# A hybrid decoder step on one core: samples' sums kept in four groups of eight rows to the end, and the first stages' expert loads issued one step later

## The reference, cut to what matters

```python
def decoder_layer(x, ...):
    mix, new_conv, new_ret = token_mixer(rmsnorm(x, norm_mix), ...)   # x @ w_in, short convolution, retention, @ w_out
    h = x + mix
    return h + moe(rmsnorm(h, norm_ffn), w_router, b_router, w_up, b_up, w_down, b_down), new_conv, new_ret

def moe(xn, ...):                       # 264 tokens, top 4 of 32 experts
    h = xb @ w_up[e] + b_up[e]          # 1024 -> 2048, rows of the tokens of expert e
    act = glu(h)                        # clamped SwiGLU
    y = act @ w_down[e] + b_down[e]     # 1024 -> 1024
    return sum over the token's 4 experts of gate * y

y_prompt = rmsnorm(hp)   # 256 prompt rows of 1024
y_sample = rmsnorm(hs)   # 8 sample rows of 1024
```

## Time and profile before

| | before |
|---|---|
| median of 3 runs | 1088.58 us |
| lowest, highest | 1085.95, 1090.34 us |
| the profiled execution | 1085.15 us |
| its span in the trace | 1083.2 us |
| TensorE busy | 1065.2 us (98%) |
| VectorE busy | 361.7 us (33%) |
| ScalarE busy | 152.6 us (14%) |
| read from HBM, written | 427.00 MB, 3.48 MB |
| mean rate over the span | 397 GB/s |

### The profile page before, as it was taken

The page is one execution under the profiler, slowest core; times in us unless marked ns, Lnnn a source line. Parts: engine busy times, 40 slices in busy tenths (PEclk is TensorE's granted clock), DMA queues, the critical chain, the costliest instruction groups (busy, mean ns, idle before and its releaser), DMA issues.

```text
span 1083.2 us, 13193 instructions
## 1 busy us (share of the span) xinstructions
PE 1065.2 (98%) x5692; PEld 446.5 (41%) x5693; DVE 361.7 (33%) x572; ACT 152.6 (14%) x302; POOL 11.9 (1%) x28
## 2 busy tenths in 40 slices
PE   9999999999999999999999999999999999999997
PEld 7888664333333333333333333333333333333332
DVE  3376534233332223333322222323332232232234
ACT  2121144101111110111111111011111101011113
POOL 1000010000000000000000000000000000000002
PEclk9999999999999999999999999999999999999999
DMA  8975949999999999999999999999999999999994
GB/s 292 312 276 198 407 161 381 412 428 426 433 434 427 433 431 430 431 429 431 433 429 428 434 431 428 430 432 431 429 430 434 430 429 430 426 427 427 430 415 177
DMA packets 40907, 431.47 MB, mean 398 GB/s; under 512 B 4456, under 2 KB 19852, under 8 KB 25104
## 3 DMA queue, kind: packets, MB, share of 16 engines
q1 hardware_dynamic: 40240, 430.41, 94.8%
q10 hardware_dynamic: 608, 0.20, 0.1%
HBM read 427.00 MB, written 3.48 MB: 397 GB/s over the span
## 4 chain that ended last, share of the span: by engine, by line
PE 83%; DMA 15%; SPq 1%; issue 0%; ACT 0%; DVE 0%; ACTq 0%; POOLq 0%; DVEq 0%; POOL 0%
PE bank L1015 37%; PE bank L1034 15%; DMA ring_all<-in_w_up 14%; PE bank L695 8%; PE bank L1079 6%; PE bank L989 4%; PE bank L1026 2%; PE bank L805 2%; PE bank L997 2%; PE bank L1007 1%; PE bank L1072 1%; PE bank L1091 1%; PE bank L813 1%; DMA ring_all<-in_w_in 1%; SPq L516 1%; PE bank L648 1%
## 5 line engine op out<-in xcount | busy, mean ns | idle before, releaser
L1015 PE MATMUL bank<-ring_all,work 128*64 128x512 f32 x2048 | 484.6, 600 | 7.7 <-DMA ring_all<-in_w_up 7.7
L1015 PEld LDWEIGHTS bank<-ring_all,work 128*64 128x64 f32 x2048 | 134.7, 136 | 257.4 <-issue 247.9
L1034 PE MATMUL bank<-ring_all,work 128*64 128x512 f32 x992 | 225.3, 596 | 0.0
L1847 DVE TENSOR_TENSOR h_tok<-h_tok,bank 128x1024 f32<-128x1024 f32 (+1 forms) x67 | 81.8, 1221 | 236.6 <-PE bank L1079 230.7
L1034 PEld LDWEIGHTS bank<-ring_all,work 128*64 128x64 f32 x992 | 68.4, 137 | 129.1 <-issue 128.2
L695 PE MATMUL bank<-work,ring_all 128*128 128x264 f32 x384 | 87.0, 387 | 1.0 <-DMA ring_all<-in_w_in 1.0
L1817 DVE TENSOR_TENSOR work<-bank,bias_up 128x1024 f32<-128x1024 f32 x32 | 39.2, 1224 | 124.0 <-PE bank L1026 124.0
L695 PEld LDWEIGHTS bank<-work,ring_all 128*128 128x128 f32 x384 | 72.5, 190 | 13.4 <-DMA ring_all<-in_w_in 1.4
L1079 PE MATMUL bank<-work 64*128 64x512 f32 (+1 forms) x268 | 75.1, 637 | 0.0
L1834 DVE TENSOR_TENSOR work<-work 128x512 f32<-128x512 f32 x32 | 22.2, 693 | 108.8 <-ACT work L1419 108.8
L1403 ACT ACTIVATE work<-bank 128x264 f32<-128x264 f32 x32 | 12.5, 390 | 315.9 <-PE bank L1007 315.9
(11 more groups left out here) (236 smaller groups left out, 549.0 us busy)
## 6 DMA issues: line engine op xcount, KB each, us to landing
ring_all<-in_w_up SPq DMA_DIRECT2D x48, 4096.0 KB, 32.8
ring_all<-in_w_down SPq DMA_DIRECT2D x24, 4096.0 KB, 33.9
ring_all<-in_w_up SPq DMA_DIRECT2D x30, 2048.0 KB, 38.1
ring_all<-in_w_down SPq DMA_DIRECT2D x13, 2048.0 KB, 40.5
ring_all<-in_w_in SPq DMA_DIRECT2D x13, 1024.0 KB, 5.1
ring_all<-in_w_down SPq DMA_DIRECT2D x6, 1024.0 KB, 21.8
ring_all<-in_w_out SPq DMA_DIRECT2D x4, 1024.0 KB, 11.7
ring_all<-in_w_up SPq DMA_DIRECT2D x4, 1024.0 KB, 6.1
```

What stands on the lines that cost most here:

```text
L1015: mm = pe.matmul(bank[half * CAP:(half + 1) * CAP, up_bank(n) + b, :].rearrange("q (k p) -> q p k", k=KT), x, src[:, half * FF + b * 512:h ...
L1034: mm = pe.matmul(bank[half * CAP:(half + 1) * CAP, Y, :], av[:, 2 * i + k, :], src[:, k * D + half * 512:k * D + (half + 1) * 512], start= ...
L1847: tt(rows, rows, bank[0:m, b:b + 2, :], ALU.add).then_inc(comb_added, 1)
```

## The change

What it does:

- SP: chunk k of the experts is issued at j = 5 + 2k instead of 3 + 2k, so chunks 0 to 5 go out at j = 5 to 15. The wait for `summed` moves with chunk 5 to j = 15, and `store_states` now stands behind chunk 5. The router's weights move to j = 5. The two b_up loads and the copy of the convolution's state move behind the whole loop.
- Samples: `FOLD` is gone. `combine`, `bias` and `combine_last` always use the form with four groups of rows, DVE adds to `sums`, and b_down's product for the samples is eight matmuls in place of two. At n = 0 eight more products with `ident` bring the samples' rows of `h_tok` into the groups.
- End: the order of the last sums is samples, tile 0, tile 1 (`LASTS`) in the second half. The samples' squares lie in four groups of rows; two products with a constant 0/1 matrix (`same_row`) add them across the groups (`join_rows`), ahead of the branch for overflow. The final norm's load is issued after chunk 186 is used and lands in that chunk's slot, with the matrix and four small pieces of the norm for the groups (`fin_in`, six DMAs). The stores are tile 0, two groups of the samples, tile 1 on SP, and two groups of the samples on ACT.

The diff, cut to its core:

```diff
@@ SP
-                    if j >= 3:
-                        k = (j - 3) // 2
-                        if j == 13:
+                    if j >= 5:
+                        k = (j - 5) // 2
+                        if j == 15:
                             sp.wait_ge(summed, 5)
-                        elif j == 15:
-                            store_states(sp)
                         if j % 2 and k < FIRST - 1:
                             sp.dma_start(ring_a[:, k, :], chunk_src(stream[k])).then_inc(landed[k], 16)
-                        if j == 3:
+                        if j == 5:
                             sp.dma_start(w_rt[:], w_router[0].rearrange("(k p) e -> p k e", p=P)).then_inc(misc_in, 16)
-                            for half, p0 in enumerate(BU):
-                                sp.dma_start(x_tok[p0:p0 + E, 2, :], b_up[0, :, half * FF:(half + 1) * FF]).then_inc(bu_in, 16)
-                            sp.dma_start(conv_sample[0, :, 0, :], state_conv[0, :, 1, :]).then_inc(out_done, 16)
+                        if j == 15:
+                            store_states(sp)
...
                 sp.dma_start(b_rt[:], b_router.partition_broadcast(P)[:, 0, :]).then_inc(b_rt_in, 16)
+                for half, p0 in enumerate(BU):
+                    sp.dma_start(x_tok[p0:p0 + E, 2, :], b_up[0, :, half * FF:(half + 1) * FF]).then_inc(bu_in, 16)
+                sp.dma_start(conv_sample[0, :, 0, :], state_conv[0, :, 1, :]).then_inc(out_done, 16)
...
-                sp.wait_ge(comb_psum, CT * (FOLD + 1))
+                sp.wait_ge(mm_done, LATE + 1)
+                sp.dma_start(same_row, c_square[:, 8, :]).then_inc(fin_in, 16)
                 sp.dma_start(g_fin[:], norm_final.rearrange("(a d) -> a d", a=1)
-                             .partition_broadcast(P)[:, 0, :]).then_inc(late_in, 16)
+                             .partition_broadcast(P)[:, 0, :]).then_inc(fin_in, 16)
+                for g in range(4):
+                    sp.dma_start(g_fold[32 * g:32 * g + NS], norm_final.rearrange("(a n g t) -> g a n t", a=1, n=2, g=4)[g]
+                                 .partition_broadcast(NS)[:, 0]).then_inc(fin_in, 16)
@@ PE, combine
-                    if c == 2 and isinstance(n, int) and n < FOLD:
+                    if c == 2:
+                        if isinstance(n, int) and n == 0:
+                            for g in range(4):
+                                for half in range(2):
+                                    pe.matmul(bank[32 * g:32 * g + 32, C + half, 0:P], ident[0:NS, 0:32],
+                                              h_tok[0:NS, 2, half * 512 + g * P:half * 512 + (g + 1) * P], start=True, stop=False)
...
-                    if fold:
-                        for half in range(2):
-                            for g in range(4):
-                                mm = pe.matmul(bank[0:m, C + half, g * P:(g + 1) * P], ident[:, 32 * g:32 * g + m],
-                                               sums[:, half, :], start=False, stop=(g == 3))
@@ PE, ahead of the branch
+                def join_rows():
+                    pe.matmul(bank[:, X, 0:1], same_row, st[:, 2:3], start=True, stop=False)
+                    pe.matmul(bank[:, X, 0:1], same_row, st[:, 5:6], start=False, stop=True).then_inc(sel_psum, 1)
...
+                pe.wait_ge(fin_in, 96)
+                pe.wait_ge(fin_part, CT)
+                pe.wait_ge(fin_sel, 1)
+                join_rows()
```

More of the change, by code:

```diff
@@ L1094, in down_last, with combine_last @@
                     return mm
-                def combine_last(p, c):
+                def combine_last(i):
+                    p, c = last_sums[i]
                     t0, m = TOK[c]
-                    i = CT + CT * p + c
-                    pe.wait_ge(comb_added, CT * (E - 2) + i - 1)
-                    if c == 0:
+                    b = CL[(i + 1) % 2]
+                    pe.wait_ge(comb_added, CT * (E - 1) + i - 1)
+                    if i % CT == 0:
                         pe.wait_ge(y_copied, E + p)
                         pe.wait_ge(spread_copied, E)
[L1104 to L1107, removed]
+                    if c == 2:
+                        for g in (0, 2, 1, 3):
+                            at = slice(g // 2 * CAP, (g // 2 + 1) * CAP)
+                            mm = pe.matmul(bank[32 * g:32 * g + 32, b, 0:P], spread[at, (E - 1) % 2, t0:t0 + 32],
+                                           y_rows[at, p * 256 + g % 2 * P:p * 256 + (g % 2 + 1) * P], start=True, stop=True)
+                    else:
+                        for half in range(2):
+                            at = slice(half * CAP, (half + 1) * CAP)
+                            mm = pe.matmul(bank[:, b + half, 0:256], spread[at, (E - 1) % 2, t0:t0 + m],
+                                           y_rows[at, p * 256:(p + 1) * 256], start=True, stop=True)
                     mm.then_inc(comb_psum, 1)
@@ L1116, in bias @@
                     for half in range(2):
-                        mm = pe.matmul(bank[0:m, C + half, :], gt[:, t0:t0 + m], b_down_sb[:, half * 512:(half + 1) * 512],
-                                       start=True, stop=True)
+                        if c == 2:
+                            for g in range(4):
+                                mm = pe.matmul(bank[32 * g:32 * g + 32, C + half, 0:P], gt[:, t0:t0 + 32],
+                                               b_down_sb[:, half * 512 + g * P:half * 512 + (g + 1) * P], start=True, stop=True)
+                        else:
+                            mm = pe.matmul(bank[:, C + half, :], gt[:, t0:t0 + m], b_down_sb[:, half * 512:(half + 1) * 512],
+                                           start=True, stop=True)
                     mm.then_inc(bias_psum, 1)
@@ L1210, in downs_last @@
                             if p == 1 and j in (1, 4):
[L1211 to L1214, removed]
+                                combine_last(j // 4)
+                    for i in range(2, 2 * CT):
+                        combine_last(i)
                 ups(0)
@@ L1939, in overflow @@
                     activate(n, None)
-                    for c in range(CT):
-                        add(CT + CT * n + c, c)
+                    for i, c in enumerate(LASTS):
+                        add(CT + CT * n + i, c)
                 def weigh_again(k):
                     dve.wait_ge(comb_added, k * CT + SUMS)
-                    dve.wait_ge(fin_weighted, CT)
-                    for c in range(CT):
+                    dve.wait_ge(fin_weighted, 2)
+                    for c in range(2):
                         ins = weigh(c)
@@ L1969, in shape_constants @@
     sq[:, 3] = 1.0
+    sq[:, 8] = np.arange(P)[:, None] % 32 == np.arange(P) % 32
     lg = np.log(f(1.0) - f(2.0) ** (f(-5.0) - np.arange(HEADS, dtype=f)))
```

184 lines of the change are left out of this document (109 added, 75 removed).

## The result

| | before | after |
|---|---|---|
| median (22 runs each) | 1088.88 us | 1091.15 us |
| lowest, highest | 1085.66, 1092.27 | 1089.65, 1092.62 |
| the profiled execution | 1085.15 | 1089.98 |
| its span | 1083.2 | 1088.2 |
| TensorE busy | 1065.2 | 1062.3 |

The ratio of after to before is 1.0025, with a 95% interval of 1.0017 to 1.0033: slower by 0.25%, within the 0.5%. The forecast was 1091.7 us and +3.1 us; measured are 1091.15 and +2.3.

A forecast was written before the change was run, and what follows sets the result against it. The prediction took the expert weight stream, set by its start and bytes, as the bound. Terms -1.0 + 5.0 - 0.6 - 0.3 = +3.1 us on 1088.58 gave 1091.7 us, range 1086.0 to 1095.2.

The forecast's parts named there:

- the first rival: Near 131 us, TensorE's clock falls in the stall, costing 2.2 us more; 1094.2 us in total, chance 0.25.
- The two rules of the expert stage: Expert stage: a shifted stream start moves the end one for one; TensorE savings ahead of 1057.6 us become waits.
- the 4.2 us of savings: Experts 26 to 29: shorter samples' products and fold save TensorE 4.2 us, counted as 0 because weight waits absorb them.
- The weight waits: Expert stage: TensorE's waits for weights add up to about 12 us in place of 8.6, mostly growing behind 965 us.
- Expert 30's product: Last expert's samples' product, behind the wait for chunk 189, gets shorter: -0.6 us.
- The late w_out piece: At `out_rows(0, 2)`, about 131 us: chunk 5 queued ahead delays w_out piece 2, so TensorE stands still, +5.0 us.
- from a stall of about 4.7 us on: Stall length near 131 us from which the clock was said to fall, taken from the end of the trace.
- The early wait: Near 40 us: TensorE's 0.97 us wait for w_in tile 4 goes away, -1.0 us.
- The tail: End of the kernel: samples' square leaves the chain's end, stores and joins add waits; bounds -0.8 and +0.7, taken -0.3 us.
- The rival without a stall: Near 131 us, w_out piece 2 isn't late, so only the gains of -1.9 us remain: 1086.7 us, chance 0.15.
- the rival of the savings: Expert stage: TensorE's 4.2 us count too, without the stall; 1082.5 us, 0.6% faster, chance 0.1.
- The range's upper end: Whole kernel: 1095.2 us, the falling-clock case of 1094.2 plus 1.0 for a tail at its slow bound.

The follow-up runs named there:

- e9: e3 with SyncE's last stores reordered, tile 1's 0.5 MB store ahead of its two stores of samples; 1085.20 us.
- e1: The kernel before with only SyncE's order of loads in the first stages changed as in the change; 1090.89 us, ratio to before 1.0022.
- e5: The kernel before, unchanged, profiled a second time; the profiled execution took 1089.34 us.
- e2: The changed kernel with SyncE's order of loads in the first stages put back as before; 1088.50 us, ratio to before 0.9997.
- e4: The changed kernel with eight unused matmuls put ahead of the wait for w_out piece 2; 1089.32 us, ratio to before 1.0012.
- e8: The kernel before with e3's whole order of SyncE's first stages, without the change's samples' part; 1084.88 us, ratio to before 0.9951.
- e7: The kernel before with only b_up's loads and the convolution state's copy moved behind the loop; 1085.42 us, ratio to before 0.9966.
- e10: e3 unchanged, run again beside e9 on the same chip; 1084.89 us, ratio to before 0.9972.
- e3: The changed kernel with chunk 5 issued behind the last w_out piece instead of ahead of the stores; 1084.19 us, ratio to before 0.9961.
- e6: The kernel before with e3's chunk order, but router's weights, b_up and the convolution state's copy left at j = 3; 1084.81 us, ratio 0.9957.

## Why the prediction was right or wrong

The time, its direction and its size came out right: 1091.7 us and +3.1 were forecast, 1091.15 and +2.3 measured. What happened, though, is the case of the first rival, the stall with the lower clock behind it, and that rival's own number, 1094.2, is 3 us too high. The forecast's number fits by luck, since two of its terms were too small and have opposite signs. By its steps:

- **The two rules of the expert stage held, within about 1 us.** The first up product is 171.81 - 167.08 = 4.7 us later, and the last expert's down product starts 1066.25 - 1061.07 = 5.2 us later, so the shift is passed on, with 0.5 us more. Between these two points stand the 4.2 us of savings that I had priced at 0, and they aren't there: the stretch is 894.0 to 895.3 us long in the six traces with the samples' part of before, and 894.4 to 895.2 in five of the six with the change's (897.0 in e9's, an execution 1.6 us above its median). The weight waits took them: 11.9 us, where I had said about 12, in place of 8.6, and 2.4 of the 3.3 us of growth lie behind 965 us. No single wait is longer, though I had expected it of the last chunks: the weight load waits 0.9 us for chunk 189 in both profiles. There are more waits.
- **Expert 30's product** gave its 0.6 us: 5.2 us late ahead of it, TensorE is 1076.40 - 1071.80 = 4.6 us late at the last down product.
- **The late w_out piece came, at its place.** I had piece 2 landing 15 to 16 us after its issue; 15.5. The term was +5.0 us, the wait is 4.2. The step that was off: 2.1 MB more ahead of the piece at 410 GB/s are 5.1 us, but allowing for the 1.2 us by which TensorE and the queue were early (131.24 - 130.02 at the matmuls ahead of the stall), its landing moved by 135.3 - 131.9 + 1.2 = 4.6 us. The store of the states behind chunk 5 took 132.5 - 127.65 = 4.8 us from the landing of the 0.25 MB ahead of it; before it was 129.2 - 123.55 = 5.65. By these landings some of the queue's time before was not the bytes' own. Why the store took 0.85 us longer before is open.
- **The clock fell.** I gave that a quarter of the chances and 2.2 us, and left it out of the sum. It fell in this profile and in e1's, at a cost of 1.7 us, and at the early wait in e5's (1.6 us) and e2's (3.0 us). The condition, "from a stall of about 4.7 us on", came from one fall at the end of the trace, and was too high: in e5 the last matmul ended at 39.1 us and the clock was down before 42, and in e4 it fell in a wait of 2.17 us. The price I had worked out from the first matmuls of the trace; they take twice as long as later ones, but the clock's column reads 1.00 there, so that the lower level held them is inferred from their times alone. The "Trainium skill", page "TensorE: Matmul & The Clock Gate", Part 1, has idleness bring back the lower level; these traces agree, and e4 shows it from the other side.
- **The early wait was priced from one execution.** -1.0 us was right for the profile at hand: there TensorE was 1.2 us early ahead of the stall, and the first up product is later by the stall and the clock less that (4.2 + 1.7 - 1.2 = 4.7). Even so the sum of 1088.3 us for that profile missed by 1.7 us, the size of the clock's term: the changed kernel's took 1089.98. For the median the -1.0 was wrong. e8 against before is -4.6 us in the same series (1084.88 and 1089.45), e7, with b_up alone moved, -4.0, and before's second profile shows 2.98 us of wait and 1.6 us of lower clock where the first had 0.97. This is the largest error in the working.
- **The tail** was to give 0.3 us and cost 0.4, within the bounds I had put. The square's place did help (the last one now starts at 1081.01, right behind tile 0's), but POOL's power ends 1082.27 + 0.96 and tile 1's store goes out at 1084.95.

So the forecast's terms in the median were about -4.5 for the early wait, +5.9 to +7 for the new stall with its clock, and -0.7 to 0 for the samples and the tail (an estimate from medians of different series): +0.7 to +2.5, against +2.3 measured. Mine were -1.0, +5.0 and -0.9. The total agrees within 1 us because two terms were too small in opposite directions: the gain by 3.5, the price by 1 to 2, most of it the clock.

The rival without a stall and the rival of the savings both fell. The range's upper end was set by the right mechanism, and the forecast should have held it; its price for the clock, 2.2 us, was a little high, since the fall at this place cost 1.7.

## What to carry to other kernels

A load that is pulled out of a busy queue goes somewhere else in the same queue: write down the order of issue with bytes and landings on both sides of the new place, and compare the slack of what stands behind it (0.3 us here) with the bytes put ahead. Ask of every wait that you price whether it is the same in each execution; a kernel that spreads over 6.6 us may have a term that the one profile doesn't show, and the spread says how large it may be. When a stall of some microseconds is forecast for TensorE, put the lower clock into the sum and not among the rivals, or fill the stall with matmuls.

## What the runs showed of the hardware

- TensorE's clock fell to its lower level after these idle times, counted from its last matmul: 2.0 us (e4, at 836 us), 2.7 (e2), 2.8 (e5), 4.4 (changed kernel: idle since 131.1, down within 135 to 136), 4.7 (end of the first profile) and 4.8 (e1). Waits of 0.88 us (e4), 0.97 (before) and 2.08 (e10) left it up, so near 2 us the length of the idleness alone doesn't decide. It was down for about 3.4 us in e1, e4, e5 and the changed kernel, at a cost of 1.6 to 1.7 us, and for 6.8 us in e2, at a cost of 3.0.
- The issue of a DMA can hold SyncE for long: b_up's two loads held it 6.43, 7.52 and 7.84 us in three executions of the same order, 3.32 us without a chunk ahead of them, and 0.89 us behind the loop. How late the next load is depends on what else it waits for: 0.1 us in the first profile, 1.4 and 1.8 in the other two.
- A wait of 0.97 to 3.4 us near 40 us, different in each execution of the same program, with the clock behind it, accounts for most of the 7 us by which executions of the kernel before differ. The four kernels without it and without the late w_out piece (e3, e6, e7, e8) spread over 0.9 to 1.7 us; e3's second series, over 2.8. Only three executions with the wait were profiled, so its length in the others is inferred from their times.
